# Sums of a norm's squares: seven additions per norm, from VectorE's queue to GpSimd's

## The reference, cut to what matters

```python
def rmsnorm(x, w):
    xf = x.astype(jnp.float32)
    y = xf * lax.rsqrt(jnp.mean(xf * xf, axis=-1, keepdims=True) + EPS)
    return (y * w.astype(jnp.float32)).astype(x.dtype)

# first layer:  x = x + mix(rmsnorm(x, norm1_w)) @ w_out
#               u = causal_dwconv(rmsnorm(x, norm2_w) @ w_up, ffn_conv_w)
#               x = x + (silu(gate) * up) @ w_down;   x = rmsnorm(x, final_norm_w)
# second layer: x = x + mix2(rms_norm(x, norm1_g)) @ w_out
#               x = x + square(relu(rms_norm(x, norm2_g) @ w_ff1)) @ w_ff2
#               out = rms_norm(x, final_g)
```

## Time and profile before

| what | value |
|---|---|
| time, median of 3 runs | 2517.07 us (2516.57 to 2520.61) |
| time of the profiled execution | 2516.36 us |
| its span, first to last instruction | 2514.6 us |
| TensorE busy | 2465.0 us, 98% |
| VectorE busy | 1510.5 us, 60% |
| ScalarE busy | 1098.6 us, 44% |
| GpSimd busy | 55.2 us, 2% |
| mean granted TensorE clock | 0.996 |

### The profile page before, as it was taken

How to read it: one execution, slowest core, us unless ns; L and a number is a source line. 1 busy time by engine, 2 the same in 40 slices (tenths; PEclk the granted TensorE clock), 3 DMA queues, 4 the chain that set the end, 5 groups by cost and what they waited for, 6 DMA issues and landing times.

```text
span 2514.6 us, 35248 instructions
## 1 busy us (share of the span) xinstructions
PE 2465.0 (98%) x13947; PEld 2025.6 (81%) x13947; DVE 1510.5 (60%) x2483; ACT 1098.6 (44%) x1783; POOL 55.2 (2%) x110
## 2 busy tenths in 40 slices
PE   7999999999999999999999999999999999999998
PEld 5888777787788888888888788787888888888887
DVE  4234546666366766656669844565888646655555
ACT  4123247776545444446444453444333433433332
POOL 0000000000000011000000000000000000000000
PEclk9999999999999999999999999999999999999999
DMA  6322330110445565565435564423323332333332
GB/s 212 104 84 84 121 118 19 61 61 19 124 122 173 193 201 188 198 209 178 141 93 185 158 193 132 153 84 93 93 84 92 101 99 86 117 106 96 98 88 82
DMA packets 318646, 304.36 MB, mean 121 GB/s; under 512 B 10271, under 2 KB 277908, under 8 KB 318356
## 3 DMA queue, kind: packets, MB, share of 16 engines
q1 hardware_dynamic: 301956, 241.30, 32.4%
q0 software_dynamic: 14400, 56.11, 5.5%
q10 hardware_dynamic: 2128, 4.72, 0.5%
HBM read 244.41 MB, written 57.67 MB: 120 GB/s over the span
## 4 chain that ended last, share of the span: by engine, by line
PE 88%; DVE 6%; ACT 2%; issue 2%; DMA 1%; SPq 0%; DVEq 0%; ACTq 0%
PE PS L2140 15%; PE PS L2142 14%; PE PS L2141 14%; PE PS L1794 11%; PE PS L2157 7%; PE PS L2159 7%; PE PS L2158 7%; PE PS L1965 3%; PE PS L2099 1%; PE PS L1951 1%; PE PS L2075 1%; PE PS L2087 1%; DVE cg L1741 1%; DVE x L1638 1%; DMA raw<-in_w_ff 1%
## 5 line engine op out<-in xcount | busy, mean ns | idle before, releaser
L2140 PE MATMUL PS<-hh,wh 128*128 128x512 f32 x1728 | 677.8, 392 | 2.4 <-DVE hl L1611 1.6
L2142 PE MATMUL PS<-hh,wl 128*128 128x512 f32 x1728 | 673.5, 390 | 0.0
L2141 PE MATMUL PS<-hl,wh 128*128 128x512 f32 x1728 | 673.1, 390 | 0.0
L960 ACT ACTIVATE wh<-raw 128x1024 fp32r<-128x1024 f32 x352 | 366.7, 1055 | 482.5 <-PE PS L2159 343.1
L1335 DVE TENSOR_TENSOR wl<-raw,wh 128x1024 fp32r<-128x1024 f32 x286 | 346.1, 1222 | 280.1 <-ACT wh L960 279.9
L1638 DVE TENSOR_TENSOR x<-x,PS 128x512 f32<-128x512 f32 x432 | 292.6, 683 | 167.3 <-PE PS L2159 166.0
L2140 PEld LDWEIGHTS PS<-hh,wh 128*128 128x128 f32 x1728 | 325.0, 188 | 71.9 <-DVE hl L1611 3.3
L2142 PEld LDWEIGHTS PS<-hh,wl 128*128 128x128 f32 x1728 | 324.8, 188 | 68.0
L2141 PEld LDWEIGHTS PS<-hl,wh 128*128 128x128 f32 x1728 | 325.1, 188 | 66.8 <-issue 0.5
L2157 PE MATMUL PS<-fh,wh 128*128 128x512 f32 x856 | 339.1, 396 | 9.0 <-DVE x L1638 8.9
L2159 PE MATMUL PS<-fh,wl 128*128 128x512 f32 x856 | 334.2, 390 | 0.0
(11 more groups left out here) (302 smaller groups left out, 2567.6 us busy)
## 6 DMA issues: line engine op xcount, KB each, us to landing
raw<-in_w_ff SPq DMA_DIRECT2D x128, 512.0 KB, 4.0
raw<-in_w_up SPq DMA_DIRECT2D x88, 512.0 KB, 4.3
wl_s<-wl POOLq DMA_DIRECT2D x66, 512.0 KB, 5.4
wl<-wl_s SPq DMA_DIRECT2D x66, 512.0 KB, 3.5
raw<-in_w_in SPq DMA_DIRECT2D x59, 512.0 KB, 3.9
raw<-in_w_down SPq DMA_DIRECT2D x44, 512.0 KB, 5.5
raw<-in_w_out SPq DMA_DIRECT2D x32, 512.0 KB, 3.9
qkvz_s<-st POOLq DMA_DIRECT2D x16, 512.0 KB, 2.9
```

The costliest lines, as they stand in the source:

```text
L960: A(whs(slot), raw[:, k % 2], ACT.Copy).then_inc(s["w_hi"], 1)
L2140: mm(bank, wh[:, k % 4, cut], hh[:, kk, span(a_)], start=kk == 0, stop=False)
L2141: mm(bank, wh[:, k % 4, cut], hl[:, kk, span(a_)], start=False, stop=False)
L2142: last = mm(bank, wl[:, k % 4, cut], hh[:, kk, span(a_)], start=False, stop=kk == KT - 1)
```

## The change

The table of the planner's VectorE times gets "acc": 0. The stage "acc" goes from VectorE's program to GpSimd's, with the same operands, waits and signal. Everything that waits for q_acc (squares, "cols", "fcols") waits for GpSimd's signal now.

```diff
 VECTOR_US = {"prep": 1.28, "high": 0, "unit": 0.45, "cdiag": 0.8, "diag": 0.8, "cols": 0.15, "cvar": 0.15, "mean": 0.15, "var": 0.15,
-             "inv": 0.15, "fcols": 0.15, "finv": 0.15, "fturn": 1.25, "spread": 0, "sq": 0, "turn": 0, "dev": 0, "sig": 0,
+             "inv": 0.15, "fcols": 0.15, "finv": 0.15, "fturn": 1.25, "spread": 0, "sq": 0, "acc": 0, "turn": 0, "dev": 0, "sig": 0,
              "v": 0, "silu": 0, "ffn2": 0, "fin2": 0, "mhi": 0}
...
                     pool.dma_start(wl_s[:, sent[k]], wl[:, k % 4].bitcast(F32)).then_inc(st_free[k % 4], 16)
+                elif stage[0] == "acc":
+                    r, k = stage[1:]
+                    pool.wait_ge(s["q_sq"], count("q_sq", "sq", r, k))
+                    if k >= 2:
+                        pool.wait_ge(s["q_acc"], count("q_acc", "acc", r, k - 1))
+                    nc.gpsimd.tensor_tensor(sums(r), sums(r), squares(r, k), ALU.add).then_inc(s["q_acc"], 1)
                 elif stage == ("clow", 0, 3):
...
-                elif name == "acc":
-                    r, k = stage[1:]
-                    dve.wait_ge(s["q_sq"], count("q_sq", "sq", r, k))
-                    if k >= 2:
-                        dve.wait_ge(s["q_acc"], count("q_acc", "acc", r, k - 1))
-                    TTo(sums(r), sums(r), squares(r, k), ALU.add).then_inc(s["q_acc"], 1)
                 elif name == "cols":
```

## The result

The changed kernel took 2543.28 us (median of 3 runs, 2541.13 to 2543.72) against 2517.07 (2516.57 to 2520.61): ratio 1.0097, 95% interval 1.0077 to 1.0117, slower by some 26 us. The forecast was 2524.5 with a range of 2517 to 2531. The sign was right, the size was not. The profiled execution took 2541.13 us, with a span of 2539.0. The kernel before was timed again with each group of experiments, at 2519.26, 2518.26 and 2519.17 us (medians of 7, 25 and 9 runs; one further run, of 3437.88 us at a mean granted clock of 0.671, is left out as slow).

What follows compares the result with a forecast made beforehand. TensorE, busy 98% of the span, was taken as the bound. Norm 3's two waits (2.6 + 2.6), clock 1.6, SBUF turns 1.0, norm 6 0.3 and tail -0.2 gave +7.9 us: 2524.5 us, range 2517 to 2531.

Steps and rivals of the forecast that it cites:

- the tail: Norm 9, at the kernel's end: GpSimd's additions keep pace with the groups and the last ends earlier, -0.2 us.
- The 0 for norms 0, 2, 4, 5, 7 and 8: At these norms a unit of 5.44 us or more ahead of "cols" hides the slower additions: 0 us.
- The order at norm 3: Six in-place scalings (fx) and squares ahead of "up"; TensorE's group wait grows 2.6 us, "cols" waits 2.6 us.
- signs of being wrong: Wrong if additions are under 0.9 or over 1.6 us, overlapped fx stretch, or norms 0-2, 4, 5, 7, 8 wait.
- norm 1 at 0: At norm 1, GpSimd's additions between sends of wl fit between two units and add no wait: 0 us.
- the clock: After norm 3's two waits, TensorE's granted clock drops for a stretch: +1.6 us, between 0 and 3.2.
- turns at SBUF: At norm 3, GpSimd additions and VectorE's fx may take turns at SBUF: +1.0 us of at most 2.3.
- Norm 6: At norm 6, "cols" comes four groups earlier and waits 1.4 us, while a 1.08 us wait goes: +0.3 us.
- The likeliest case: At norm 3, square and GpSimd addition hold ScalarE's queue and "cols" waits: 2521 to 2529 us, chance 0.58.
- The third rival: Slow or contended GpSimd, 1.9 us per addition, costing at norms 3 and 6, clock and tail: +18, 2534 us, chance 0.14.
- The second rival: Quick GpSimd, 0.7 us per addition, with the clock staying full: +1.8, 2518 us (2516 to 2521), chance 0.22.
- the fourth (faster): VectorE's freed 45 us shorten TensorE's 8.9 us of bank waits and clock loss: up to -6, 2511 us, chance 0.06.

Runs made afterwards that it cites:

- selective: Kernel before, its planner list kept, with only the 49 additions outside norms 1, 3 and 6 moved to GpSimd: 2519.81 us, ratio 1.0003.
- write_only: Changed kernel with norm 3's seven additions left out and GpSimd writes of about their length in their place: 2541.7 us, one run.
- order_only: Kernel before with "acc": 0 in the planner's table and all additions still on VectorE: 2535.3 us, ratio 1.0064.
- send_later: Changed kernel with each GpSimd send of wl held until the next weights' stage, behind the addition: 2539.11 us, ratio 1.0075.
- gaps: Kernel before with eleven waits of rising length put into TensorE's queue in the last layer: 2573.18 us, one run.

## Why the prediction was wrong

**Right, or nearly.** The length of an addition: 1.26 to 1.30 us alone. But the prediction's 1.3 was to be the distance from one to the next, and dependent additions start 1.43 us apart (2518.99, 2520.42, ... in the tail), so they don't quite keep pace with groups of 1.36: the tail was -0.2 forecast and +0.25 measured. The 0 for norms 0, 2, 4, 5, 7 and 8: nothing there but 0.48 us at norm 5, and `selective` shows no cost of these additions that a time can tell. VectorE's freed time brought nothing. The order at norm 3, and its 4.3 us wait without the hindrance (4.26 in `write_only`); that `order_only` waits 4.20 with all additions on VectorE shows that the same delay needs no GpSimd. Two of the prediction's own signs of being wrong came: the fx stretched, and a wait came at norm 1.

**The step that failed outright** is norm 1 at 0: "nothing new is waited for, with 5.44 us between two units the sends and additions (1.9 us) fit". I added up busy time on GpSimd, and it is true that the addition had stood behind the subtraction before. What counts is the ring, and that its turn grew from 4.4 to 5.1 us by the send and the longer addition: an addition behind a send waits for a subtraction, which waits for a rounding, which stands behind a square that waits for the addition before. Measured 3.77 us of wait and 6.7 us in all; `send_later` takes the wait away without moving an addition off GpSimd.

**Mis-sized: the clock.** Forecast 1.6 of at most 3.2 us, measured 9.5. I let two waits of one norm cost one stretch each. There were three norms with long waits, and around those of 3.77, 2.85 and 6.21 us lay 6.8, 6.8 and 10.2 us at half clock, where the one row I had showed 3.4; in `gaps` three of the four waits from 4.72 us on had 6.8. So a part of this follows from the missed waits, and a part from taking the single stretch of before as the price.

**Mis-sized: turns at SBUF.** Forecast 1.0 of at most 2.3. `write_only` gives 1.95 us at the group wait alone, and 2.3, the upper end, was the better choice. My working counted the fx that meet additions, and neither the product for "up" (1.38 for 0.75) nor the subtractions of other stages (two of wl in 3.10 us at norm 6, where the same two took 2.36 before).

**Overlooked at norm 3:** the 2.19 us at 1221.80. I followed "cols" up to its own wait, and not what the earlier norm packs ahead of the next unit. Against that, "cols" waited 1.54 for the forecast 2.6: acc 7 ended at G + 4.5 (G is again the end of the first group's addition), but the group ahead of "cols" ran at half clock, so TensorE came at G + 3.0 and not at G + 1.4. Together the waits of norm 3 are 8.3 us for 5.2 forecast.

**Norm 6:** forecast +0.3, measured 2.25 of waits and 3.1 of clock. Fx 7 stands behind a subtraction of wl that waited for a rounding on ScalarE and ran 1.40 us long, and it started only when TensorE had come to "cols" (1703.40 and 1703.34), where I had it start 1.35 us earlier. So "cols" waited 2.85 for 1.4. In `order_only` it waited 4.06: this wait is the order's, too.

Sum by the prediction's terms, measured: norm 1 3.8, norm 3 8.3, norm 6 2.25, tail 0.25, clock 9.5, start 0.4: 24.5 for the 24.4 us of span (the turns are inside the waits). The likeliest case named two waits that did come, 6.21 - 1.67 and 1.54 us, a quarter of the whole; most of the rest stood in none of its terms, or at a small part of its size. The third rival, slow or contended (2534), had the contention, but put it down to additions of 1.9 us, and they are slow only where they meet VectorE. The second rival (0.7 us) is refuted by the durations, the fourth (faster) by the changed kernel itself and by `selective`.

Open: why the stretches at half clock differ by 3.4 us between kernels with the same waits (10.2 and 13.6 us at norm 3). The runs show that it happens, not what decides it.

## What to carry to other kernels

When work moves to an idle engine, follow its queue and not its busy share: ask of each moved instruction what stands ahead of it, what that waits for, and whether this leads back to the instruction's own result. A price of 0 in a planner's table moves everything behind it, and here that alone cost more than the slower engine. If TensorE is the bound, a long stall can be paid again in clock (here each of 3.5 us and more had half clock around it, and those whose price could be read cost 1.3 us and more on top), so one missed wait is worth several small gains elsewhere.

## What the runs showed of the hardware that was not expected

- GpSimd and VectorE block each other both ways, and the blocked time is counted in the instruction: GpSimd's addition 1.26 to 1.30 us alone and up to 2.24 beside VectorE, fx 0.68 and 1.02 (mean of six), a product of two buffers 0.75 and 1.38 to 1.67, two subtractions of wl 3.10 together for 2.36. A blocked product ended 0.55 us after the addition that it met. Fills on GpSimd of 1.19 us did not slow the fx. So a busy share read from such a profile is too high by the blocked time: VectorE lost 48 us of work and 32.9 us of busy time.
- TensorE's clock was at half for 3.4 or 6.8 us around waits of 3.55 us and more in `gaps`, which cost 1.3 to 2.5 us beyond the wait, and full behind 2.97, but at half also behind a 2.73 us wait.
